# Running the seams between the dense stages of a transformer layer in two token halves, with three weight tiles taken together at the start of the next stage

## The chip, the cores and the metric

The kernel runs on one core of a Trainium2 chip. The metric is the device time of one execution in microseconds (us). TensorE (PE) multiplies, VectorE (DVE), ScalarE (ACT) and GpSimd (POOL) do the elementwise work, and SyncE (SP) issues most of the DMAs.

## The reference

One layer of a decoder for 512 prompt tokens and 8 sampled tokens, 520 in all, with a model width of 1024:

```python
hp = half_ffn(yp, *ffn1)                                    # stage a
... project(rmsnorm(hp, g_mix_pre), w_in, ...)              # 23 projection tiles
... fox_attention, nsa_attention (prompt and paged samples)
hp = hp + rmsnorm(merge_groups(o_fox, o_nsa, g_fox, g_nsa, w_out), g_mix_post)   # stage b
yp = half_ffn(hp, *ffn2)                                    # stage c

def half_ffn(x, g_pre, wg, wu, wd, g_post):
    return x + 0.5 * rmsnorm(swiglu(rmsnorm(x, g_pre), wg, wu, wd), g_post)
def swiglu(x, wg, wu, wd):
    return (silu(x @ wg) * (x @ wu)) @ wd
def rmsnorm(x, g):
    return x * rsqrt(mean(x * x) + EPS) * g
```

Everything is float32. So each dense stage ends with a norm over the whole width of its output, a sum into the residual, and a second norm ahead of the next stage's products.

## The kernel before

**Layout.** The width lies on the partitions: `H` (the residual), `Y` (a stage's output) and the operand tiles are 8 tiles (`KT`) of 128 partitions by 520 tokens (`TOK`). One matmul takes `HALF` = 260 tokens, since a PSUM bank holds 512 floats; `ps[:, 0:8]` are the eight banks, and slot n of `halves(n)` is the pair of banks 2n and 2n+1.

**Split operands.** Each float32 product is made of three: operand and weight are each split in a high and a low part (`XH`, `XL` or `UH`, `UL`; `WH`, `WL`), and `products` does, for each of the tiles `kt`, high by high, low by high and high by low, each for both halves of the tokens: 6 matmuls per `kt`, 48 for an item of eight `kt`.

**Items.** The weights come as items of 128 output columns. SP reads two items per DMA (1 MB) into `RAW`, which has two slots; ScalarE copies an item to `WH` (the high part) and VectorE subtracts to `WL` (the low part). `WH` and `WL` have two buffers each. `split(k)` is ScalarE's or VectorE's part of that for item k, and waits for semaphore `items_used` to reach k-1. SP issues a DMA when both items of the slot that it overwrites have been split by both engines. The items are counted through the program: FFN 1, the projections from `IT_PROJ` (23 items, the first of them the gates, "fg", the next four the queries, "fq"), the output projection from `IT_OUT` (8), FFN 2 from `IT_F2`.

**Order.** Each engine has its own program, written out by hand and linked by semaphores. In an FFN, gate and up items ("gu") alternate, then "down" tiles sum over the hidden units in two groups of 12 and 10; the last down tile of the second group is 2 items of 5 `kt`, 60 matmuls.

**A seam**, before the change: PE ends the last output tile (t = 7) of the stage. VectorE adds it into `Y` (in stage b three operations that scale two partial sums), ScalarE squares it (`SQ`) and scales it by the gain (`finished`), PE sums the squares of the seven earlier tiles (`ACC`) and of this one over the partitions by float32 matmuls with `ones` (`output_squares`), and ScalarE makes the token's factor of it by Ln and Exp (`rstd`, into `GT`). Then, tile by tile: VectorE `UT = Y * GT` (line 988), `H = H + UT` (line 992), ScalarE `XH` (line 668) and the square of `H` (line 670), VectorE `XL` (line 968), PE the first item's products for that `kt`, as soon as `XL` is there. The squares of `H` are summed by PE too (`first_operands`, `token_squares`), and give `token_rstd` (`R1`), by which the results of the next stage are scaled as they leave PSUM. While ScalarE and VectorE prepare, PE does 28 matmuls whose result nobody reads (`keep_warm(WARM[1])`). Behind stage c there is no next stage: `H` goes out as `y` by DMAs on ScalarE's queue.

The seams are called a (FFN 1 to projections), b (output projection to FFN 2) and c (the end).

**Start of the projections.** The gates' tile needs Sigmoid, Exp and Ln on ScalarE with a load of the function table ahead of each; ScalarE does these between the splits of items `IT_PROJ`+3 and +4, in `late_part(0)` and `softplus`.

## Time and profile before

| | |
|---|---|
| time, median of 3 runs | 1227.45 us (1222.09 to 1432.55) |
| time of the profiled execution | 1222.94 us |
| its span, first to last instruction | 1221.1 us |
| PE busy | 1171.5 us, 96% |
| DVE, ACT, POOL busy | 536.5, 419.2, 146.8 us |
| mean granted clock of TensorE | 0.978 |

The profile is of one execution. Its times are counted from the first instruction; a row of the timeline gives start, duration, engine, line, operation, what it writes and reads, and in brackets the idle time ahead of it with what ended it. `x2` joins two instructions in a row. `SPq` is SyncE's queue of DMAs. The granted clock is 1.00 at 2.4 GHz and 0.50 at 1.2 GHz.

### The profile page before, as it was taken

How to read it: one execution, taken by the hardware profiler on the slowest of the kernel's cores; microseconds unless marked ns; L12 is line 12 of the kernel's file. 1: busy time of each engine (PE TensorE's matmuls, PEld its weight loads, DVE VectorE, ACT ScalarE, POOL GpSimd, SP SyncE). 2: the span in 40 equal slices, each digit the busy share in tenths (PEclk: the TensorE clock that was granted, in tenths of full speed). 3: DMA queues.
4: the chain of work that ended last, by engine and by line, in shares of the span. 5: the costliest groups of instructions: out<-in, count | busy, mean ns of one | idle time of the engine just before them, and what ended most of it. 6: DMA issues, size and time to landing. Idle time of an engine off the chain costs nothing.

```text
span 1221.1 us, 23231 instructions
## 1 busy us (share of the span) xinstructions
PE 1171.5 (96%) x9460; PEld 1081.3 (89%) x9466; DVE 536.5 (44%) x772; ACT 419.2 (34%) x731; POOL 146.8 (12%) x150
## 2 busy tenths in 40 slices
PE   9999999999999899998979899989999999999994
PEld 6999999999999799996546556969999999999994
DVE  4433422343333644364465766574334333333334
ACT  6322322222234542234433555453223212223342
POOL 0101100001111000122212311210111000011110
PEclk9999999999999999999998898999999999999997
DMA  6322223322223133314762211222222223222221
GB/s 276 104 71 101 87 78 100 116 70 103 79 69 122 48 118 124 105 70 123 167 181 79 104 70 36 70 69 70 76 97 94 78 78 130 70 104 90 66 87 70
DMA packets 49008, 117.53 MB, mean 96 GB/s; under 512 B 8186, under 2 KB 24954, under 8 KB 43138
## 3 DMA queue, kind: packets, MB, share of 16 engines
q1 hardware_dynamic: 45746, 110.55, 27.6%
q10 hardware_dynamic: 3184, 5.88, 1.3%
q8 instruction: 56, 0.92, 0.3%
q14 instruction: 22, 0.18, 0.0%
HBM read 107.79 MB, written 7.97 MB: 95 GB/s over the span
## 4 chain that ended last, share of the span: by engine, by line
PE 91%; DVE 5%; issue 2%; ACT 2%; DMA 0%; DVEq 0%; SPq 0%; ACTq 0%
PE ps L1472 73%; PE ps L1879 4%; PE ps L1599 3%; PE ps L1632 2%; PE ps L1616 2%; PE ps L1481 2%; PE ps L1666 1%; DVE UT L988 1%; DVE H L992 1%; DVE row_max L1146 1%; PE ps L1607 1%; DVE PTS L486 1%; PE ps L1565 1%; DMA RAW<-in_w_gu 0%; ACT PRB L823 0%
## 5 line engine op out<-in xcount | busy, mean ns | idle before, releaser
L1472 PE MATMUL ps<-XH,WH 128*128 128x260 f32 x1776 | 364.2, 286 | 6.6 <-DVE XL L968 6.6
L1472 PE MATMUL ps<-XH,WL 128*128 128x260 f32 x1776 | 358.2, 283 | 0.0
L1472 PE MATMUL ps<-XL,WH 128*128 128x260 f32 x1776 | 357.7, 283 | 0.0
L417 ACT CAST WH<-RAW 128x1024 fp32r<-128x1024 f32 (+2 forms) x183 | 175.0, 956 | 519.8 <-PE ps L1472 500.5
L1472 PEld LDWEIGHTS ps<-XH,WH 128*128 128x128 f32 x1776 | 276.1, 189 | 11.1 <-DVE XL L968 8.2
L1472 PEld LDWEIGHTS ps<-XH,WL 128*128 128x128 f32 x1776 | 274.2, 189 | 0.0
L1472 PEld LDWEIGHTS ps<-XL,WH 128*128 128x128 f32 x1776 | 273.6, 189 | 0.0
L420 DVE TENSOR_TENSOR WL<-RAW,WH 128x1024 fp32r<-128x1024 f32 (+2 forms) x183 | 203.7, 1113 | 154.1 <-ACT WH L417 152.8
L1472 PE MATMUL ps<-UL,WH 128*128 128x260 f32 x704 | 141.8, 283 | 0.0
L1472 PE MATMUL ps<-UH,WL 128*128 128x260 f32 x704 | 141.5, 282 | 0.0
L1472 PE MATMUL ps<-UH,WH 128*128 128x260 f32 x704 | 141.3, 282 | 0.0
L1377 POOL TENSOR_TENSOR UL<-HT,UH 128x520 f32 (+1 forms) x44 | 57.6, 1310 | 634.2 <-ACT UH L699 634.2
L1472 PEld LDWEIGHTS ps<-UH,WL 128*128 128x128 f32 x704 | 108.5, 188 | 0.0
L1472 PEld LDWEIGHTS ps<-UH,WH 128*128 128x128 f32 x704 | 108.5, 188 | 0.0
L1472 PEld LDWEIGHTS ps<-UL,WH 128*128 128x128 f32 x704 | 108.4, 188 | 0.0
L1008 DVE TENSOR_TENSOR UT<-ps,token_rstd 128x520 f32<-128x520 f32 x44 | 30.8, 699 | 145.8 <-PE ps L1472 145.8
L1004 DVE TENSOR_TENSOR GT<-ps,token_rstd 128x520 f32<-128x520 f32 x44 | 30.8, 699 | 129.6 <-PE ps L1472 119.8
L699 ACT CAST UH<-HT 128x520 f32 (+1 forms) x44 | 27.6, 627 | 86.1 <-DVE HT L1015 86.1
L1121 DVE TENSOR_TENSOR TR<-ps,token_rstd 128x520 f32<-128x520 f32 x23 | 16.1, 700 | 68.0 <-PE ps L1472 44.6
L1146 DVE TENSOR_REDUCE row_max<-ps 128x2 f32<-128x256 f32 (+3 forms) x48 | 39.2, 817 | 11.5 <-PE ps L1607 11.4
L823 ACT ACTIVATE PRB<-ps,row_max 128x384 f32<-128x384 f32 (+1 forms) x48 | 30.0, 629 | 27.0 <-DVE row_max L1146 27.0
L486 DVE COPY PTS<-ps 128x128 f32<-128x128 f32 (+3 forms) x48 | 23.4, 488 | 31.7 <-PE ps L1616 25.9
(250 smaller groups left out, 1063.8 us busy)
## 6 DMA issues: line engine op xcount, KB each, us to landing
RAW<-in_w_gu SPq DMA_DIRECT2D x44, 1024.0 KB, 4.8
RAW<-in_w_down SPq DMA_DIRECT2D x16, 768.0 KB, 4.5
RAW<-in_w_in SPq DMA_DIRECT2D x11, 1024.0 KB, 4.8
RAW<-in_w_down SPq DMA_DIRECT2D x16, 640.0 KB, 4.3
KF<-in_fox_k SPq DMA_DIRECT2D x16, 256.0 KB, 4.2
VF<-in_fox_v SPq DMA_DIRECT2D x16, 256.0 KB, 4.0
RAW<-in_w_out SPq DMA_DIRECT2D x4, 1024.0 KB, 4.9
H<-in_x SPq DMA_DIRECT2D x4, 520.0 KB, 6.9
```

What stands on the lines that cost most here:

```text
L417: nc.scalar.copy(WH[:, par, 0:width], RAW[:, slot, j, 0:width]).then_inc(w_hi, 1)
L420: nc.vector.tensor_tensor(WL[:, par, 0:width], RAW[:, slot, j, 0:width], WH[:, par, 0:width], ALU.subtract).then_inc(w_lo, 1)
L486: copy(PTS[:, w % PT_SLOTS, 0:i + 1, :], ps[:, 4 + w % 2, 0:P * (i + 1)].rearrange("p (a n) -> p a n", n=P)).then_inc(sem(name), 1)
L699: nc.scalar.copy(row(UH, st.m), HT[:, st.par, :]).then_inc(sem("hid_hi"), 1)
L823: nc.scalar.activation(weights(v)[:, 0:W], ps[:, score_bank(v), 0:W], ACT.Exp, bias=row_max[:, v:v + 1], accum_out=row_sum[:, v:v + 1]).th ...
L1004: nc.vector.tensor_tensor(two(GT[:, st.par, :]), halves(0), two(R1[:, :]), ALU.mult).then_inc(sem("evac"), 1)
L1008: nc.vector.tensor_tensor(two(UT[:, st.par, :]), halves(1), two(R1[:, :]), ALU.mult).then_inc(sem("evac"), 1)
L1146: nc.vector.reduce_max(row_max[:, v:v + 2], ps[:, score_bank(v):score_bank(v) + 2, 0:W], AX.X, negate=True).then_inc(sem("att_max"), 1)
L1377: nc.gpsimd.tensor_tensor(row(UL, st.m), HT[:, st.par, :], row(UH, st.m), ALU.subtract).then_inc(sem("hid_lo"), 1)
L1472: q = nc.tensor.matmul(ps[:, 2 * slot + half, 0:HALF], w[:, par, cols], x[:, kt0 + kt, half * HALF:(half + 1) * HALF], start=first and kt ...
L1599: nc.tensor.matmul(ps[:, score_bank(v + j), 0:W], QX[part, h // 2, i * P:i * P + P], KX[part, k, 0:W], start=True, stop=False, skip_group_ ...
L1879: q = nc.tensor.matmul(ps[:, 2 * slot + half, 0:HALF], w[:, (IT_OUT + t) % 2, cols], x[:, kt, half * HALF:(half + 1) * HALF], start=kt % 4 ...
```

## The change

At each of the three seams the last output tile is multiplied for the first 260 tokens and then for the other 260 (before: both halves alternate). VectorE, ScalarE and PE do everything behind it for each half apart: add, square, the sum over the partitions (`half_sums`), Ln and Exp, `UT`, `H`, `XH`, square, `XL`. The next stage takes its first three items together, operand by operand: for a half h and a tile kt, nine matmuls, three for each item (`border_products`), in banks 0 to 3, 6 and 7; the items are split into three extra pairs of buffers (`EH`, `EL`), which lie where nothing lives at that time, ahead of the seam. Item +3 is split in the second half of the seam, item +4 behind it. The 28 idle matmuls at seams a and b go. `y` goes out in 16 halves on SP's queue instead of 8 tiles on ScalarE's. `OR`, `OU` and `late` move to other addresses.

```diff
+        def border(k):
+            for first in (IT_PROJ, IT_F2):
+                if isinstance(k, int) and first <= k < first + 5:
+                    return k - first
+            return None
...
             def write(k, par, slot, count, j, width):
-                if not isinstance(k, int) or k >= 2:
+                if border(k) is not None:
+                    eng.wait_ge(used, k - border(k) - (0, 0, 0, 0, 1)[border(k)] - (4 if border(k) < 3 else 0))
+                elif not isinstance(k, int) or k >= 2:
                     eng.wait_ge(used, k - 1)
...
             def behind(f, s, e):
+                if f == 1 and s.kind == "gu" and s.g == 0 and s.number == 0:
+                    return
                 if s.number is not None:
                     item(IT_F[f] + 2 * s.M + 2 + e)
+                    if f == 0 and s.M == FFN_STEPS - 1 and e == 1:
+                        item(IT_PROJ + 2)
                     return
...
@@ SyncE
-            sp.wait_ge(sem("y_stored"), 16 * KT)
+            for h in (0, 1):
+                for t in range(KT):
+                    sp.wait_ge(sem("mixed"), since("mixed", "c", h * KT + t + 1))
+                    sp.dma_start(O["y"][:, t, columns(h)], H[:, t, columns(h)]).then_inc(sem("y_stored"), 16)
...
@@ ScalarE
             def after(s, name):
-                rstd(s, "yss", 4 if s in "ac" else 1, GT[:, 0, :], "yrstd")
+                half_finished(s, 0)
+                half_rstd(s, 0, "yss", factor, GT[:, 0, :], "yrstd")
                 if name is None:
+                    half_finished(s, 1)
+                    half_rstd(s, 1, "yss", factor, GT[:, 0, :], "yrstd")
                     return
-                operands(s, name, lambda t: act.wait_ge(sem("mixed"), since("mixed", s, t + 1)))
+                for h in (0, 1):
+                    for t in range(KT):
+                        act.wait_ge(sem("mixed"), since("mixed", s, h * KT + t + 1))
+                        nc.scalar.activation(XH[:, t, columns(h)], H[:, t, columns(h)], ACT.Copy,
+                                             scale=gain(name, t)).then_inc(sem("xhi"), 1)
+                        nc.scalar.activation(Y[:, t, columns(h)], H[:, t, columns(h)], ACT.Square).then_inc(
+                            sem("hsq"), 1)
+                        if h == 0 and t == 1:
+                            half_finished(s, 1)
+                        elif h == 0 and t == 5:
+                            half_rstd(s, 1, "yss", factor, GT[:, 0, :], "yrstd")
+                        elif h == 1 and t == 3:
+                            split(first + 3)
+                        elif h == 1 and t == 5:
+                            half_rstd(s, 0, "hss", 1, R1[:, :], "rstd")
+                half_rstd(s, 1, "hss", 1, R1[:, :], "rstd")
...
             def project():
                 for j in range(NPROJ):
-                    if j + 2 < NPROJ:
+                    if 2 <= j < NPROJ - 2:
                         split(IT_PROJ + j + 2)
...
@@ VectorE
             def after(s, name):
+                last_out(s, 0)
+                for h in (0, 1):
+                    c, n = columns(h), h * KT
+                    dve.wait_ge(sem("yrstd"), since("yrstd", s, h + 1))
+                    for t in range(KT + 2):
...
+                        if h == 0 and t == 2:
+                            last_out(s, 1)
...
+                        if h == 1 and t == 7 and name:
+                            split(first + 3)
...
-            for t in range(KT):
+            for t in range(KT - 1):
                 dve.wait_ge(used, IT_OUT + t + 1)
...
                 split(IT_OUT + t + 2)
+            split(IT_F2 + 1)
+            split(IT_F2 + 2)
             after("b", "ffn2_pre")
...
@@ TensorE
+            def half_sums(s, h):
+                bank, c = ps[:, 4 + h, 0:HALF], columns(h)
+                if h == 0:
+                    pe.wait_ge(sem("acc"), since("acc", s, KT - 1))
+                pe.wait_ge(sem("ysq"), since("ysq", s, KT + h))
+                nc.tensor.matmul(bank, ones, ACC[:, c], start=True, stop=False)
+                nc.tensor.matmul(bank, ones, SQ[:, (KT - 1) % 2, c], start=False, stop=True).then_inc(sem("yss"), 1)
+            def border_products(s, first):
+                for n in range(3):
+                    ready(first + n)
+                for h in (0, 1):
+                    for kt in range(KT):
+                        pe.wait_ge(sem("xlo"), since("xlo", s, h * KT + kt + 1))
+                        for n in range(3 if h == 0 or kt < 4 else 2):
+                            q = part(n, kt, h)
+                            if h == 1 and kt == KT - 1:
+                                q.then_inc(used, 1)
+                        if kt >= KT - HSQ_PE:
+                            t = kt - (KT - HSQ_PE)
+                            nc.tensor.matmul(ps[:, 4 + h, 0:HALF], ones, Y[:, t, columns(h)], start=t == 0, stop=False)
+                        if h == 1 and kt == 2:
+                            half_token_squares(s, 0)
+                for kt in range(4, KT):
+                    q = part(2, kt, 1)
+                q.then_inc(used, 1)
+                half_token_squares(s, 1)
...
+                    if st.g == 1 and known == KT - 1:
+                        for h in (0, 1):
+                            for e in (0, 1):
...
+                                if h == 1:
+                                    q.then_inc(used, 1)
+                                    if e == 0:
+                                        half_sums(s, 0)
+                            if h == 0:
+                                q.then_inc(sem("half_done"), 1)
+                        half_sums(s, 1)
...
-            keep_warm(WARM[1])
...
             def project():
-                for j in range(NPROJ):
+                border_products("a", IT_PROJ)
+                pe.wait_ge(sem("projected"), 2)
+                turn(0)
+                for j in range(3, NPROJ):
```

What the change does to the order of the instructions, at the places where the engines wait for each other. ScalarE at seam a before; the first row is the split of the last two down items, the two `WH` rows of 1024 are `IT_PROJ` and +1, and rows 659 and 662 are Ln and Exp:

```order
L417 CAST WH<-RAW 128x640 [waits w_raw1,items_used] x2
L647 ACTIVATE SQ<-Y 128x520 [waits acc,evac]
L651 ACTIVATE Y<-Y,gains 128x520 [waits ysq]
L417 CAST WH<-RAW 128x1024 [waits w_raw0,items_used]
L647 ACTIVATE SQ<-Y 128x520 [waits acc,evac]
L651 ACTIVATE Y<-Y,gains 128x520 [waits ysq]
L417 CAST WH<-RAW 128x1024 [waits w_raw0,items_used]
L659 ACTIVATE ST<-ps,consts 128x520 [waits yss]
L662 ACTIVATE GT<-ST 128x520 [waits yss_ln]
```

ScalarE at the same place after (`EH_81`, `EH_83` and `EH_85` are the high parts of `IT_PROJ`, +1 and +2):

```order
L451 CAST WH<-RAW 128x640 [waits w_raw1,items_used] x2
L689 ACTIVATE SQ<-Y 128x520 [waits acc,evac]
L693 ACTIVATE Y<-Y,gains 128x520 [waits ysq]
L451 CAST EH_81<-RAW 128x1024 [waits w_raw0,items_used]
L451 CAST EH_83<-RAW 128x1024 [waits w_raw0,items_used]
L451 CAST EH_85<-RAW 128x1024 [waits w_raw1,items_used]
L730 ACTIVATE SQ<-Y 128x260 [waits acc,last_out]
L733 ACTIVATE Y<-Y,gains 128x260 [waits ysq]
L718 ACTIVATE ST<-ps,consts 128x260 [waits yss]
L721 ACTIVATE GT<-ST 128x260 [waits yss_ln]
```

The split of item +2 now stands ahead of the square of the last tile, and waits for another slot of `RAW` than its two neighbours. VectorE at the same place after:

```order
L454 TENSOR_TENSOR WL<-RAW,WH 128x640 [waits w_hi,items_used]
L454 TENSOR_TENSOR EL_82<-RAW,EH_81 128x1024 [waits w_hi,items_used]
L454 TENSOR_TENSOR EL_84<-RAW,EH_83 128x1024 [waits w_hi,items_used]
L454 TENSOR_TENSOR EL_86<-RAW,EH_85 128x1024 [waits w_hi,items_used]
L1072 TENSOR_TENSOR Y<-Y,ps 128x260 [waits half_done]
L1087 TENSOR_TENSOR UT<-Y,GT 128x260 [waits yg,yrstd]
L1087 TENSOR_TENSOR UT<-Y,GT 128x260 [waits yg]
L1091 TENSOR_TENSOR H<-H,UT 128x260 [waits normed]
L1087 TENSOR_TENSOR UT<-Y,GT 128x260 [waits mixed,yg]
L1091 TENSOR_TENSOR H<-H,UT 128x260 [waits normed]
L1072 TENSOR_TENSOR Y<-Y,ps 128x260 [waits items_used]
L1097 SCALAR_TENSOR_TENSOR XL<-H,gains,XH 128x260 [waits xhi]
```

The three low parts stand ahead of the sum into the last tile's first half (the first row of line 1072); the second half's is the other row of line 1072. TensorE after, at the end of the last down tile of FFN 1 and the start of the three items:

```order
L1630 MATMUL ps<-ACC,consts 128x260 [waits ysq,acc]
L1631 MATMUL ps<-SQ,consts 128x260
L1636 MATMUL ps<-UH,WH 128x260
...
L1636 MATMUL ps<-UH,WL 128x260
L1630 MATMUL ps<-ACC,consts 128x260 [waits ysq]
L1631 MATMUL ps<-SQ,consts 128x260
L1636 MATMUL ps<-XH,EH_81 128x260 [waits w_hi,w_lo,xlo]
L1636 MATMUL ps<-XL,EH_81 128x260
L1636 MATMUL ps<-XH,EL_82 128x260
L1636 MATMUL ps<-XH,EH_83 128x260
```

The sum of the first half's squares stands ahead of the last 15 of the tile's 60 matmuls, and the second half's ahead of the next stage.

## Rows read from the trace of the kernel before

**Rows 1.** The page, part 4: the chain that ended last, share by engine.

```profile
PE 91%; DVE 5%; issue 2%; ACT 2%; DMA 0%; DVEq 0%; SPq 0%; ACTq 0%
```

**Rows 2.** The chain in order of time: start, duration, what.

```profile
423.23 0.88 PE ps L1481 x4
...
428.85 51.88 PE ps L1472 x432
...
830.37 373.07 PE ps L1472 x3108
```

**Rows 3.** Timeline, seam a.

```profile
393.18 0.37 SPq L507 DMA_DIRECT2D RAW<-in_w_in  x1
...
398.21 0.40 PE L1472 MATMUL ps<-UH,WL 128*128 128x260 f32 x2
...
400.14 1.14 PE L1481 MATMUL ps<-SQ,consts 128*128 128x260 f32 x4 [0.65 <-ACT SQ L647]
...
402.41 0.64 ACT L662 ACTIVATE GT<-ST 128x520 f32<-128x520 f32 x1
403.08 1.31 DVE L988 TENSOR_TENSOR UT<-Y,GT 128x520 f32<-128x520 f32 x2
```

**Rows 4.** DMAs, KB and median us from issue to landing: 392 to 400 us, and the page.

```profile
RAW<-in_w_in SPq DMA_DIRECT2D x1, 1024.0 KB, 6.1
...
RAW<-in_w_in SPq DMA_DIRECT2D x11, 1024.0 KB, 4.8
```

**Rows 5.** Timelines of ACT and DVE, start of the projections.

```profile
429.45 0.63 ACT L730 ACTIVATE QXF<-TR 128x512 f32<-128x512 f32 x1
...
435.84 1.05 ACT L417 CAST WH<-RAW 128x1024 fp32r<-128x1024 f32 x1
...
437.00 1.23 DVE L420 TENSOR_TENSOR WL<-RAW,WH 128x1024 fp32r<-128x1024 f32 x1 [1.66 <-ACT WH L417]
```

**Rows 6.** Timelines of SP, DVE and ACT, seam b.

```profile
784.00 11.87 SPq L507 DMA_DIRECT2D RAW<-in_w_gu  x2
...
800.00 1.22 DVE L420 TENSOR_TENSOR WL<-RAW,WH 128x1024 fp32r<-128x1024 f32 x1
...
800.79 0.73 ACT L651 ACTIVATE Y<-Y,gains 128x520 f32<-128x520 f32 x1
```

**Rows 7.** Timeline, seam c.

```profile
1203.03 0.40 PE L1472 MATMUL ps<-UH,WL 128*128 128x260 f32 x2
...
1207.53 1.31 DVE L988 TENSOR_TENSOR UT<-Y,GT 128x520 f32<-128x520 f32 x2 [3.30 <-ACT GT L662]
1208.76 0.69 DVE L992 TENSOR_TENSOR H<-H,UT 128x520 f32<-128x520 f32 x1
...
1217.25 1.30 DVE L992 TENSOR_TENSOR H<-H,UT 128x520 f32<-128x520 f32 x2
```

**Rows 8.** Groups by line and form: count, busy us, mean ns, idle before.

```profile
L968 DVE SCALAR_TENSOR_TENSOR XL<-H,gains,XH 128x520 fp32r<-128x520 f32 x24 | 18.0, 757 | 2.5 <-ACT XH L668 2.3
...
L486 DVE COPY PTS<-ps 128x512 f32<-128x512 f32 x12 | 8.3, 691 | 15.4 <-PE ps L1616 15.4
...
L486 DVE COPY PTS<-ps 128x256 f32<-128x256 f32 x12 | 5.0, 417 | 1.7 <-PE ps L1616 1.7
...
L823 ACT ACTIVATE PRB<-ps,row_max 128x512 f32<-128x512 f32 x24 | 16.3, 682 | 17.1 <-DVE row_max L1146 17.1
...
L823 ACT ACTIVATE PRA<-ps,row_max 128x256 f32<-128x256 f32 x24 | 11.1, 469 | 6.1 <-DVE row_max L1146 6.0
```

**Rows 9.** Windows: length, busy PE, PEld, DVE, ACT, POOL, then PEclk, DMA share, GB/s.

```profile
412.90:416.20 3.30, 3.30 (x12) 2.91 (x13) 3.30 (x6) 2.03 (x4) 0.00 (x0) 0.50 0.00 0
...
803.80:805.90 2.10, 0.00 (x0) 0.00 (x0) 2.05 (x4) 1.06 (x2) 0.00 (x0) 1.00 0.00 0
...
1206.10:1208.20 2.10, 0.00 (x0) 0.00 (x0) 0.67 (x2) 1.33 (x2) 0.00 (x0) 1.00 0.00 0
1208.20:1221.10 12.90, 0.00 (x0) 0.00 (x0) 9.73 (x16) 0.00 (x0) 0.00 (x0) 0.50 0.43 165
```

More of the change, by code:

```diff
@@ L671, in operands, with half_rstd @@
                 rstd(s, "hss", 1, R1[:, :], "rstd")
+            def half_rstd(s, h, kind, factor, dst, done):
+                act.wait_ge(sem(kind), since(kind, s, h + 1))
+                e = 1 if factor == 4 else 0
+                nc.scalar.activation(ST[:, 0, columns(h)], ps[:, 4 + h, 0:HALF], ACT.Ln, scale=factor / D_MODEL,
+                                     bias=const("eps")[:, e:e + 1]).then_inc(sem(kind + "_ln"), 1)
+                act.wait_ge(sem(kind + "_ln"), since(kind + "_ln", s, h + 1))
+                nc.scalar.activation(dst[:, columns(h)], ST[:, 0, columns(h)], ACT.Exp, scale=-0.5).then_inc(
+                    sem(done), 1)
@@ new lines, in half_product, with part @@
+            def half_product(hi, lo, col, x, kt, bank, h, start, stop):
+                cols = slice(col * P, col * P + P)
+                for p, (w, v) in enumerate(((hi, XH if x else UH), (hi, XL if x else UL), (lo, XH if x else UH))):
+                    q = nc.tensor.matmul(ps[:, bank, 0:HALF], w[:, cols], v[:, kt, columns(h)],
+                                         start=start and p == 0, stop=stop and p == 2)
+                return q
+            def border_products(s, first):
+                tiles = [weight_tiles(first + n, None) for n in range(3)]
+                def part(n, kt, h):
+                    return half_product(*tiles[n], kt, True, kt, 2 * (0, 1, 3)[n] + h, h, kt == 0, kt == KT - 1)
+                for n in range(3):
[16 more added lines that the diff above has]
+                half_token_squares(s, 1)
@@ L1512, in ffn, with half_token_squares @@
+            def half_token_squares(s, h):
+                pe.wait_ge(sem("hacc"), since("hacc", s, h + 1))
+                nc.tensor.matmul(ps[:, 4 + h, 0:HALF], ones, Y[:, HSQ_PE, columns(h)], start=False, stop=True).then_inc(
+                    sem("hss"), 1)
             def ffn(f, before, s):
```

188 lines of the change are left out of this document (131 added, 57 removed).

## The prediction

> **What bounds the kernel now.** The chain of waits comes first: 91% of it is TensorE [rows 1], and behind each seam it runs unbroken, 432 matmuls in 51.88 us and 3108 in 373.07 us, 0.120 us each [rows 2]. So outside the seams nothing can be won, and a seam is worth what TensorE idles or does for nothing there. The reader then takes the timeline of each seam. Seam a: the last product ends at 398.6, the factor is there at 403.08, when VectorE starts on UT [rows 3], and the third item starts at 428.6, the fifth 96 matmuls later at 440.1. Seam b: TensorE stops at 803.8 [rows 9], and the 3108 matmuls hold 36 of the second item and 48 of the third, so the fourth item starts at 840.1 (the chain dates a matmul some 0.3 us behind its start). Seam c: the last product ends at 1203.4, the last H at 1218.55 [rows 7], and 2.5 us later the span ends.
>
> **Prices of half operations.** From 512 to 256 columns a VectorE copy goes from 691 to 417 ns and an ACT operation from 682 to 469 ns [rows 8]. So half of 520 columns costs 0.27 us less on VectorE and 0.22 less on ScalarE: 0.43 for UT or H (0.70 in full), 0.49 for XL. In a queue without a wait the next VectorE operation starts some 0.08 us before the last one's end, so half operations follow at 0.35 (XL 0.40). A sum over the partitions is four float32 rows in 0.88 us [rows 2], half of one is 0.44. From the end of the sums over Ln and Exp to UT it took 1207.53 - 1206.1 = 1.43 us at seam c [rows 7, 9]; with half operations 0.44 less, 1.0.
>
> **Seam a, up to the factor.** Item +2 is now split ahead of the last tile's first half, on ScalarE and on VectorE. Its DMA was issued at 393.18 [rows 3], when the last down items had been split, which the change leaves as it is; it took 6.1 us, to 399.3, where eleven of its kind have a median of 4.8 [rows 4], to 398.0. Copy 1.05 us, the low part 0.1 behind it for 1.23 [rows 5], then the half sum into Y: 402.0; the square: 402.5. The first half's 30 matmuls had ended at 395.0 and 15 more at 396.8; there TensorE stands at the sum of the squares until 402.5, with 15 matmuls queued behind. In the 12.9 us without matmuls at the end the clock was at 0.50 from 2.1 us on [rows 9], so I take it as fallen: the two half sums take 1.7 us, not 0.88. Factor at 404.2 + 1.0 = 405.2, against 403.08. The overlap that the halves would give is eaten by the split ahead of them.
>
> **Seam a, from the factor to the fifth item.** Counted from the factor: VectorE reaches the second half's sum at 1.9, ScalarE squares it behind two tiles of XH and squares at 3.15, TensorE sums until 4.1 and starts the three items. They are 144 matmuls of 0.120 (17.2), eight half sums (3.5) and two (0.9): 25.7. VectorE needs 0.35 + 0.35 + 0.40 = 1.10 us for a tile of a half where TensorE uses 1.08 to 1.5, and it starts first, so it hides behind TensorE; without that cover each 0.1 us too much costs 1.6. Then Ln and Exp (1.0) and the two full evacuations (0.62 and 0.70): 28.0. TensorE waits there for both, 2.4 us of a new wait. Then the fourth item runs, but the fifth needs ScalarE, which has the table loads of the gates' tile in front of its split: from QXF at 429.45 to the end of the low part at 438.2 it is 8.8 us [rows 5]. Before, that began early enough; now the fourth item's 5.7 and 0.5 for the turn are over at 6.2 and TensorE stands 2.7 us. The fifth item starts at 405.2 + 28.0 + 8.9 = 442.1 against 440.1: **+2.0 us**. With the landing of 4.8 and the full clock it is 2.0 - 1.3 - 0.8 = -0.1.
>
> **Seam b.** The weights for +2 were issued at 795.5 [rows 6], so the DMA is no matter. ScalarE's gain copy of tile 6 starts at 800.79 [rows 6]; behind it copies of +1 and +2, and VectorE's low parts end at 803.8 and 804.9; then three half operations to 806.15, the square to 806.6. TensorE stands at the sum from 802.3 (12 matmuls left of 48) to 806.6, and again I take the sums at the low clock, 1.7: factor at 809.3. The second half's sum is three operations, 0.45 more than at a, and nothing stands in the way of the fifth item here: the fourth starts 28.5 behind the factor, at 837.8, against 840.1: **-2.3 us**. At the full clock -3.1.
>
> **Seam c.** No weights are split. Half 0 ends at 1203.4 - 3.6 = 1199.8, its square is there before TensorE has done 15 more matmuls (1201.6); sums 1202.5, factor 1203.5, 4.0 earlier than UT at 1207.53 [rows 7]. But the tail is VectorE's: H repeats every (1217.25 - 1208.76) / 6 = 1.41 us, in halves every 1.41 - 0.54 = 0.87, and there are twice as many. 15 steps and the last H are 13.5 us: 1217.0 against 1218.55, **-1.6 us**. The DMA behind the last H is half as large and on another queue; I take its 2.5 us as they were (between -0.4 and +0.5).
>
> The Trainium skill ("VectorE: DVE Perf Modes", section "The TRN2 errata — SBUF-src ops pay a fixed extra latency per instruction") says that this latency is paid between instructions and asks for tiles of at least 512 elements, which speaks against halving. The rows show a fixed part of 0.14 us (417 ns less 256 times 1.07 [rows 8]), and the 0.87 has it in; were there none, the 16 added operations at seam c would cost 2.2 us less.
>
> **Hidden.** y on SP's queue: 16 issues of 0.37 us [rows 3] at 0.87 distance. late comes behind the second half's rstd, and is read at the eighth item only. The moved buffers cost nothing. The 28 removed matmuls lay in a wait.
>
> **The sum.** 2.0 - 2.3 - 1.6 = -1.9 us, from 1222.94 of the profiled execution: 1221.0. The clock is left: the fall at 412.9 cost 3.3 us at 0.50 [rows 9], that is 1.7 us where TensorE is the bound, and now it is from the first matmul of the three items. TensorE idles again 1.6 and 2.7 us ahead of the three items at a and b, 2.4 behind them, and 2.7 ahead of the fifth at a. Of gaps of 2.1 us one let the clock stand and one ended with it falling [rows 9]. So one such fall is as likely as none, and between 1221.0 and 1222.7 I say **1222 us**. The runs shown have 1222.09 and 1227.45 around the profiled 1222.94, so a median may lie some us above.
>
> **Rivals.**
> - *Slower: the clock.* Two to four falls instead of one, each 3.3 us at half speed on three-item products that TensorE bounds: +3.4 to +6.8 on 1221.0, 1224.4 to 1227.8. It is slower than before from the second fall on (1.9 / 1.7). For it: the keep-warm matmuls are gone and four gaps of 1.6 to 2.7 us stand in their place. Against it: the gap of 2.1 us at 803.8 left it at 1.00 [rows 9]. 0.22.
> - The Trainium skill's rule ("TensorE: Matmul & The Clock Gate", section "Why this matters for your kernels") is to leave no long idle gap between bursts of matmuls, since the array falls to half its clock; by it this rival is the likelier one.
> - *Better: early weights or full clock.* Landing as in the median and sums at 1.00: -0.1 - 3.1 - 1.6 = -4.8, 1218.1. For it: 4.8 is the median [rows 4]. Against: this very DMA took 6.1, and both gaps are over 4 us. 0.18.
> - *The halves overlap in full:* if the splits did not stand ahead, the factor would come at 398.7 at a (-4.4 for the fifth item) and 804.5 at b (-7.1), with c's -1.6: -13.1, 1210. The orders of ScalarE and VectorE speak against it. 0.04.
> - *It doesn't do what it says:* matmuls that change weights each time instead of every second one run at more than 0.120 us. 456 of them at 0.14 are +9, 1230. Against: each matmul has its own weight load already. 0.04.
>
> **How the numbers follow.** Forecast 0.50, with a range of its own of 1219 to 1225, a change of -4 to +2 us, so of either sign; 0.02 is left for what I have not thought of. 8 in 10 need the slower and the better case too: 1214 to 1229, with some us for the scatter of the runs. 2%, 24 us, is about what a measurement of this kernel can tell from no change; no case but mishaps reaches it: faster 0.02, same 0.94, slower 0.04.
>
> **What would show it.** At a: EH/EL of item +2 ends near 401.7, UT near 405, TensorE idle from 396.8 to 402.5 behind ysq, the fourth item near 433.7, the fifth at 442.1 after a wait of 2.7 us for the low part. At b: UT near 809, fourth item near 838, the granted clock at 1.00 but for the sums and one stretch at most. At c: UT at 1203.5 less what a and b gave, steps of 0.87. Wrong if XL, not TensorE, sets the pace of the three items, if item +2 lands before 396, or if the clock falls more than once.

## The result, and the profile after

The changed kernel takes 1225.49 us (median of 20 runs, 1223.04 to 1228.61) against 1223.1 us before, a ratio of 1.0025 with a 95% interval of 1.0014 to 1.0036: it is slower by 3.1 us (1.7 to 4.4), where 0.9 us faster than the profiled execution was forecast. The 1223.1 is the median of 20 runs, four of them stray ones of 1433 to 5646 us, and the ratio leaves these four out. In a second series beside other kernels the ratio was 1.0030 (1.0018 to 1.0042).

The profiled execution has a span of 1225.7 us against 1221.1, so 4.6 us are to be found in it. The chain of waits cuts the span at places that both kernels have (start, duration, what); its lines answer to those of [rows 2]:

```profile
393.24 6.41 DMA RAW<-in_w_in
...
443.69 40.60 PE ps L1590 x336
...
765.53 37.49 PE ps L2064 x312
...
846.33 356.02 PE ps L1590 x2964
```

The 336 matmuls are the fifth to the eleventh item of the projections and end at 484.29; before, the block of 432 in [rows 2] ends at 480.73 with the same item. (For the fourth item of the kernels of before I take the place 9.7 us behind the start of the 3108, where [rows 2] and 840.1 have it.) The 312 begin the output projection behind attention, the 2964 begin with the fourth item behind seam b (840.1 before). Subtracting gives four stretches, here for every profile of the study, the experiments below included; the last two columns are the time against the kernel before as measured over all runs, and its ratio with the interval. Where two kernels are compared below over all runs, it is by the difference of their ratios, and that carries both intervals: some 2.5 us either way, and 3 to 4 where one of the last two orders (six runs each) takes part.

| kernel | to item 11 (seam a) | attention | seam b | to the end (seam c) | span | all runs, us | ratio |
|---|---|---|---|---|---|---|---|
| before | 480.7 | 279.8 | 79.6 | 381.0 | 1221.1 | | |
| changed | 484.3 | 281.2 | 80.8 | 379.4 | 1225.7 | +3.1 | 1.0025 [1.0014, 1.0036] |
| changed, again | 485.6 | 281.1 | 80.8 | 379.4 | 1226.9 | +3.7 | 1.0030 [1.0018, 1.0042] |
| warm in all four waits | 483.0 | 279.3 | 77.2 | 380.7 | 1220.1 | -1.8 | 0.9985 [0.9969, 1.0001] |
| third tile split later | 479.9 | 281.2 | 78.4 | 380.9 | 1220.3 | -3.7 | 0.9970 [0.9952, 0.9988] |
| before, without warm matmuls | 481.1 | 278.2 | 78.9 | 381.0 | 1219.2 | -1.2 | 0.9990 [0.9974, 1.0005] |
| fifth item split early, first try | 484.6 | 277.7 | 79.6 | 380.7 | 1222.6 | +2.6 | 1.0021 [1.0006, 1.0035] |
| the same, second try | 482.7 | 275.8 | 79.6 | 380.9 | 1218.9 | -1.6 | 0.9987 [0.9971, 1.0003] |
| order mended | 477.2 | 279.8 | 77.1 | 379.4 | 1213.5 | -7.8 | 0.9936 [0.9912, 0.9959] |
| order mended, warm | 476.2 | 277.9 | 74.3 | 379.4 | 1207.7 | -15.4 | 0.9874 [0.9851, 0.9898] |
| seam c in full width | 483.9 | 281.3 | 80.8 | 380.9 | 1226.9 | +4.6 | 1.0038 [1.0021, 1.0054] |
| warm in b's first wait | 483.6 | 277.9 | 78.7 | 380.8 | 1221.0 | +1.1 | 1.0009 [0.9991, 1.0026] |
| warm in b's second wait | 483.9 | 277.8 | 78.1 | 379.4 | 1219.2 | +1.2 | 1.0010 [0.9996, 1.0024] |

So in the profiles seam a costs 3.6 us, seam b 1.2, seam c gives 1.6, and attention, in which the change does nothing, has 1.4 more in this execution. The predicted terms were +2.0, -2.3, -1.6, and up to 1.7 for one fall of the clock.

**Seam a.** Timelines of the changed kernel, ScalarE, VectorE and TensorE, which answer to [rows 3] (start, duration, engine, line, operation, in brackets the idle time before it and who ended it):

```profile
399.73 1.04 ACT L451 CAST EH<-RAW 128x1024 fp32r<-128x1024 f32 x1 [4.13 <-DMA RAW<-in_w_in]
402.47 0.42 ACT L730 ACTIVATE SQ<-Y 128x260 f32<-128x260 f32 x1 [1.70 <-DVE Y L1072]
...
400.87 1.23 DVE L454 TENSOR_TENSOR EL<-RAW,EH 128x1024 fp32r<-128x1024 f32 x1 [3.76 <-ACT EH L451]
402.02 0.42 DVE L1072 TENSOR_TENSOR Y<-Y,ps 128x260 f32<-128x260 f32 x1
...
403.03 1.21 PE L1630 MATMUL ps<-ACC,consts 128*128 128x260 f32 x2 [5.87 <-ACT SQ L730]
409.31 0.70 PE L1630 MATMUL ps<-ACC,consts 128*128 128x260 f32 x2 [1.13 <-ACT SQ L730]
...
406.11 0.77 DVE L1087 TENSOR_TENSOR UT<-Y,GT 128x260 f32<-128x260 f32 x2 [3.67 <-ACT GT L721]
```

Both engines stand in front of the third item's weights until 399.7. Only behind its copy and its low part comes the half sum, though the half had been multiplied at about 395; TensorE idles 5.9 us with the rest of the tile queued behind the sum. UT comes at 406.11 against 403.08 in [rows 3]. The second halves of the seam, which answer to [rows 5]:

```profile
433.12 1.43 DVE L1235 TENSOR_TENSOR TR<-ps,token_rstd 128x520 f32<-128x520 f32 x2 [4.29 <-ACT token_rstd L721]
...
442.20 1.23 DVE L454 TENSOR_TENSOR WL<-RAW,WH 128x1024 fp32r<-128x1024 f32 x1 [5.68 <-ACT WH L451]
```

VectorE waits for the factor from 428.8, evacuates, and the low part of the fifth item ends at 443.4, where the block of 336 begins.

**Seam b.** TensorE's two waits for the squares, and the granted clock in windows (length, busy PE, PEld, DVE, ACT, POOL, PEclk, DMA share, GB/s), which answer to the second window of [rows 9]:

```profile
811.66 1.20 PE L1630 MATMUL ps<-ACC,consts 128*128 128x260 f32 x2 [4.33 <-ACT SQ L730]
818.35 1.23 PE L1630 MATMUL ps<-ACC,consts 128*128 128x260 f32 x2 [2.03 <-ACT SQ L730]
```

```profile
807.30:810.80 3.50, 0.03 (x1) 0.00 (x0) 3.21 (x5) 1.10 (x2) 0.08 (x1) 0.97 0.26 35
810.80:824.20 13.40, 10.52 (x39) 9.46 (x40) 9.38 (x26) 8.84 (x22) 0.00 (x0) 0.50 0.17 70
824.20:828.00 3.80, 3.80 (x31) 3.74 (x31) 3.36 (x8) 1.46 (x5) 0.00 (x0) 0.99 0.00 0
```

This is the reading that the prediction missed. The clock falls some 1 us before the end of the first wait and stays at 0.50 for the 13.4 us of the middle window (13.6 with its edges): through the first sums and the rest of the tile, which are 4.6 us of unbroken work, the second wait, the second sums and over 4 us of the three items. It need not look like this in every execution. Both profiled ones of the changed kernel have a mean clock of 0.970, and of its 20 runs 15 have 0.973 to 0.977; another course of the clock with the same instructions is shown below, at the two waits.

**Seam c**, against [rows 7]:

```profile
1209.88 0.77 DVE L1087 TENSOR_TENSOR UT<-Y,GT 128x260 f32<-128x260 f32 x2 [3.20 <-ACT GT L721]
...
1212.12 0.42 DVE L1087 TENSOR_TENSOR UT<-Y,GT 128x260 f32<-128x260 f32 x1
...
1212.99 0.43 DVE L1087 TENSOR_TENSOR UT<-Y,GT 128x260 f32<-128x260 f32 x1
1213.33 0.42 DVE L1091 TENSOR_TENSOR H<-H,UT 128x260 f32<-128x260 f32 x1
1213.86 0.43 DVE L1087 TENSOR_TENSOR UT<-Y,GT 128x260 f32<-128x260 f32 x1
...
1222.62 0.76 DVE L1091 TENSOR_TENSOR H<-H,UT 128x260 f32<-128x260 f32 x2
```

Steps of 0.87 us (1212.12, 1212.99, 1213.86), the last H at 1223.38. Seam b's fourth item was 6.2 us later than before; 1217.0 + 6.2 = 1223.2 was forecast.

### The profile page after: what moved, and what is told of

Its sections match the earlier page's. It is cut to its first block, busy times and chain, and to the rows that moved or that the text cites. A ratio compares the mean times of both kernels' runs of the same rounds, so it can differ in the third digit from the quotient of the medians.

```text
span 1225.7 us, 23281 instructions
## 1 busy us (share of the span) xinstructions
PE 1166.3 (95%) x9410; PEld 1080.8 (88%) x9410; DVE 543.9 (44%) x845; ACT 427.3 (35%) x779; POOL 146.8 (12%) x150
## 4 chain that ended last, share of the span: by engine, by line
PE 88%; DVE 5%; ACT 2%; issue 2%; DMA 1%; DVEq 0%; SPq 0%; ACTq 0%
PE ps L1590 68%; PE ps L1636 3%; PE ps L2064 3%; PE ps L1784 2%; PE ps L1817 2%; PE ps L1801 2%; PE ps L1851 1%; DVE row_max L1262 1%; DVE UT L1087 1%; DVE PTS L524 1%; PE ps L1658 1%; PE ps L1599 1%; DVE H L1091 1%; DMA RAW<-in_w_in 1%; DVE PRB L508 1%
## 5 line engine op out<-in xcount | busy, mean ns | idle before, releaser
L1590 PE MATMUL ps<-XH,WH 128*128 128x260 f32 x1680 | 341.7, 285 | 6.0 <-DVE UT L1119 2.5
L1590 PE MATMUL ps<-XH,WL 128*128 128x260 f32 x1680 | 339.0, 283 | 0.0
L1590 PE MATMUL ps<-XL,WH 128*128 128x260 f32 x1680 | 338.6, 283 | 0.0
L1590 PEld LDWEIGHTS ps<-XH,WH 128*128 128x128 f32 x1680 | 260.3, 189 | 8.4 <-issue 5.9
L454 DVE TENSOR_TENSOR WL<-RAW,WH 128x1024 fp32r<-128x1024 f32 (+2 forms) x177 | 196.5, 1110 | 152.6 <-ACT WH L451 151.3
L1590 PEld LDWEIGHTS ps<-XH,WL 128*128 128x128 f32 x1680 | 259.6, 189 | 0.0
L1590 PEld LDWEIGHTS ps<-XL,WH 128*128 128x128 f32 x1680 | 259.0, 189 | 0.0
L1590 PE MATMUL ps<-UL,WH 128*128 128x260 f32 x664 | 133.8, 283 | 0.0
L1590 PE MATMUL ps<-UH,WL 128*128 128x260 f32 x664 | 133.4, 282 | 0.0
L1590 PE MATMUL ps<-UH,WH 128*128 128x260 f32 x664 | 133.3, 282 | 0.0
L1262 DVE TENSOR_REDUCE row_max<-ps 128x2 f32<-128x256 f32 (+3 forms) x48 | 39.1, 816 | 13.1 <-PE ps L1792 13.0
```

The lines of the kernel that those rows point to most:

```text
L454: nc.vector.tensor_tensor(lo[:, 0:width], RAW[:, slot, j, 0:width], hi[:, 0:width], ALU.subtract).then_inc(w_lo, 1)
L1262: nc.vector.reduce_max(row_max[:, v:v + 2], ps[:, score_bank(v):score_bank(v) + 2, 0:W], AX.X, negate=True).then_inc(sem("att_max"), 1)
L1590: q = nc.tensor.matmul(ps[:, 2 * slot + half, 0:HALF], w[:, par, cols], x[:, kt0 + kt, half * HALF:(half + 1) * HALF], start=first and kt ...
```

## The experiments

Theories: **L**, the clock: TensorE's work between the waits runs at half speed, and it is TensorE that sets the pace there. **S**, the split: the third weight tile stands in front of the first half's sum and eats the overlap. **W**: the wait for the fifth item behind seam a. Each experiment's edit is against the changed kernel, but for the one that starts from the kernel before. Keep-warm matmuls are products of zeros, 128x512 in bf16, into a bank that nobody reads.

### The clock: warm matmuls in all four waits

```diff
+    keep_warm(26 if f == 0 else 0)    # ahead of half_sums(s, 0)
+    keep_warm(5 if f == 0 else 0)     # ahead of half_sums(s, 1)
+    keep_warm(19)                     # ahead of half_sums("b", 0)
+    keep_warm(8, 3)                   # ahead of half_sums("b", 1)
```

> The changed kernel with keep-warm matmuls (128x512 bf16 of zeros, 0.213 us each at full clock) put into TensorE's four waits for the squares of the last tile: 26 and 5 at seam a, 19 and 8 at seam b. Theory L (the missing time is TensorE's clock, low through bursts that stand 2 to 4 us apart): granted clock 1.00 in both sets of sums and in the three items behind them, so the UT of seam a comes 0.9 us earlier and that of seam b 0.8, the second sums of seam b 0.9 earlier and the three items there end some 2 us earlier; about 5 us less than the changed kernel (1225.5), 1220 to 1221, some 2 us below the kernel before. Rival (the clock costs nothing that another wait would not take): the same as the changed kernel within 1 us.

Measured: 4.9 us less than the changed kernel (ratios 0.9985 and 1.0025, so 2.5 to 7.3), as theory L had it, and within the uncertainty of the kernel before. The chain and a window of it:

```profile
762.23 37.51 PE ps L2066 x312
...
839.39 357.36 PE ps L1590 x2964
```

```profile
804.00:820.00 16.00, 14.26 (x88) 10.38 (x87) 12.59 (x30) 10.00 (x24) 0.10 (x1) 1.00 0.20 68
```

Seam b takes 839.39 - 762.23 = 77.2 us, 3.6 less, at a clock of 1.00 throughout. Seam a gains 1.3. The block of 2964 takes 357.36 instead of 356.02: now the clock falls at the end of the wait ahead of the fourth item, in which no warm matmul stands, and 1.3 us are given back. So the seams give 4.9 us in the profile and keep 3.6 of them. Attention has 2.0 less, which need not be the warm matmuls' doing (below).

### Which of b's two waits

```diff
+    keep_warm(19)                     # one kernel: ahead of half_sums("b", 0) alone
+    keep_warm(8, 3)                   # the other: ahead of half_sums("b", 1) alone
```

> The changed kernel with keep-warm matmuls at seam b alone, 19 of them in the first wait (for the squares of the first half), none in the second. If the first gap of 4.3 us is what lets the clock fall and the short work behind it is only too little to raise it again: the granted clock is 1.00 from 804 to 820, the sums take 0.9 instead of 2.1 us and the three items run at full clock, so the fourth item comes some 3.6 us earlier than in the changed kernel, as in the run with all waits filled. If each gap counts by itself: the clock falls at the second gap of 1.5 to 2 us instead, and the gain is 1 to 2 us.

> The changed kernel with 8 keep-warm matmuls at seam b alone, in the second wait (for the squares of the second half), none in the first. If uninterrupted work raises the clock again whatever came before: it rises soon behind the second sums, and the three items gain up to 2.1 us; the first sums stay at 0.50. Rival: the low stretch lasts as long as in the changed kernel (13 us) and the gain is under 0.5 us.

The first of them, windows (columns as above):

```profile
810.00:814.40 4.40, 1.21 (x7) 0.90 (x5) 4.26 (x13) 2.98 (x7) 0.00 (x0) 0.98 0.01 2
814.40:817.70 3.30, 3.30 (x16) 3.23 (x15) 3.30 (x10) 2.53 (x8) 0.00 (x0) 0.50 0.00 0
817.70:824.00 6.30, 6.30 (x51) 6.18 (x50) 5.65 (x15) 3.88 (x12) 0.00 (x0) 1.00 0.01 4
```

and the second:

```profile
803.60:807.80 4.20, 0.00 (x0) 0.00 (x0) 3.46 (x5) 1.48 (x4) 0.01 (x1) 0.97 0.36 90
807.80:811.00 3.20, 3.12 (x10) 2.76 (x11) 0.05 (x1) 1.38 (x3) 0.00 (x0) 0.50 0.50 210
811.00:820.00 9.00, 8.08 (x57) 6.71 (x56) 8.86 (x25) 6.60 (x17) 0.00 (x0) 1.00 0.01 2
```

With the first wait filled the clock stands there. It falls just behind the second wait, which had grown to 3.2 us since the rest of the tile now ran at full speed; the low window is 3.3 us. Seam b gains 2.1 us, but the clock falls once more at the fourth item (the block of 2964 takes 357.50), which gives 1.4 back. With the second wait filled the low window is 3.2 us, b gains 2.7, and nothing is given back.

This looks as if the second gap had held the clock down in the changed kernel. The rows do not bear that out. The first of the eight warm matmuls starts behind the rise of the clock at 811.0 (TensorE's timeline):

```profile
811.75 1.90 PE L1606 MATMUL ps<-cumb 128*128 128x512 bf16 x8
```

Up to there the instructions are those of the changed kernel, whose clock stayed down through the same burst. And the two kernels with the fifth item split early (below) have the changed kernel's instructions at seam b, without any warm matmul, and almost its waits. Windows of the first of them:

```profile
808.10:811.30 3.20, 2.89 (x9) 2.54 (x10) 0.00 (x0) 1.43 (x4) 0.00 (x0) 0.50 0.55 233
811.50:814.70 3.20, 0.91 (x8) 0.70 (x6) 3.06 (x9) 1.71 (x5) 0.00 (x0) 1.00 0.01 3
815.00:818.20 3.20, 3.10 (x10) 2.71 (x11) 3.20 (x10) 2.54 (x7) 0.00 (x0) 0.50 0.00 0
```

The clock rises in the first burst, falls again at the end of the second wait, and a third time at the fourth item (357.52 for the 2964). So the same order has had one low stretch of 13.6 us, in three profiles (the changed kernel twice and the one with seam c in full width, 80.8 us at b each), and three short ones, in two profiles (79.6 each). From the start of the 312 to the last instruction both come to the same: 460.2 us for both profiles of the changed kernel, 460.3 and 460.5 for the other two. What decides between them is open. What the filled waits show is their price: over the same stretch 457.9 us with both filled, 459.5 with the first alone, 457.4 with the second alone. Over all runs the two kernels are 2.0 and 1.8 us below the changed kernel, or 2.6 and 2.4 below its repetition beside them. Their ratios do not tell them apart.

### The split in front of the first half

```diff
 def behind(f, s, e):
-    if f == 0 and s.M == FFN_STEPS - 1 and e == 1:
-        item(IT_PROJ + 2)
 # ScalarE, after(), behind half_rstd(s, 0, "yss", ...)
+    split(first + 2)
 # VectorE, after(), behind last_out(s, 1)
+    if name:
+        split(first + 2)
 # both engines, ahead of after("b", ...)
-    split(IT_F2 + 2)
```

> The changed kernel with the third weight tile of each border split behind the first half instead of ahead of it: on ScalarE right behind the Exp of the first half, on VectorE behind the second half sum. Theory S (the split ahead of the first half ate the overlap): UT of seam a at 399.8 to 400.5 instead of 406.1, of seam b some 4.9 us earlier; the fifth item of seam a 5 to 6 us earlier; together 8 to 11 us less than the changed kernel, 1214 to 1217. Rival (the three items only start when the third tile is there and VectorE is late with its low halves, since 2.3 us of split stand among them): less than 4 us of gain, with TensorE idle behind the third tile or behind XL.

VectorE's and TensorE's timelines at seam a:

```profile
400.12 0.77 DVE L1085 TENSOR_TENSOR UT<-Y,GT 128x260 f32<-128x260 f32 x2 [2.71 <-ACT GT L719]
...
398.00 0.68 PE L1629 MATMUL ps<-ACC,consts 128*128 128x260 f32 x2 [0.92 <-ACT SQ L728]
403.32 1.13 PE L1629 MATMUL ps<-ACC,consts 128*128 128x260 f32 x2 [2.41 <-ACT SQ L728]
```

At seam a UT comes at 400.12, 6.0 us earlier: theory S holds. Of these 6.0, 4.4 are left at the eleventh item, 2.4 us come at seam b, and 1.5 are lost at the fourth item behind it, where the clock falls once more; over all runs it is 6.7 us less than the changed kernel, short of the 8 to 11. At b my 4.9 was wrong: VectorE's low part of the second item still waited for ScalarE's copy in front of the half sum, and UT came only 1.3 us earlier, counted from the 312. The missing 1.6 us at a are the clock again. The changed kernel spends its low stretch on the last 15 matmuls of the tile, in front of a wait; here it falls just behind the wait of 2.41 us and lies on the second sums (1.13 for two that take 0.70) and the first of the three items, where TensorE is the bound.

### The warm matmuls that the change removed

```diff
     ffn(0, "0", "a")
-    keep_warm(WARM[1])
...
-    keep_warm(WARM[1])
     ffn(1, "b", "c")
```

> The kernel before without its two sets of 28 keep-warm matmuls behind the sums. Theory L (their absence lets the clock fall): the first items behind the seams run at 0.50 for a stretch of at least 3 us, +1.5 to +4 us on the kernel before. Rival (they lay in a wait and cost nothing to remove): within 1 us of it.

Measured 0.9990, 1.2 us less than the kernel before with an interval from -3.2 to +0.6: their removal has no cost that shows. Yet the clock falls, and for long (a window, columns as above, and rows of TensorE's timeline in it):

```profile
403.80:416.60 12.80, 8.72 (x31) 7.47 (x32) 12.70 (x22) 8.19 (x14) 0.00 (x0) 0.50 0.24 82
```

```profile
409.07 0.80 PE L1472 MATMUL ps<-XH,WH 128*128 128x260 f32 x2 [0.16 <-DVE XL L968]
410.96 0.80 PE L1472 MATMUL ps<-XH,WH 128*128 128x260 f32 x2 [0.22 <-DVE XL L968]
412.85 0.80 PE L1472 MATMUL ps<-XH,WH 128*128 128x260 f32 x2 [0.22 <-DVE XL L968]
```

Here VectorE is busy for 12.70 of the 12.80 us, TensorE for 8.72: it takes a tile of operands when VectorE brings one, every 1.89 us, and has time left even at 0.50. The third item starts at 429.24 against 428.85 in [rows 2]. In the changed kernel a low stretch on the three items does cost, since TensorE has three items for each operand there and is busy without a pause: the change took away the slack in which a slow clock had been free.

### The wait for the fifth item

```diff
 # ScalarE, project(): ahead of the wait for the first evacuation
-    if 2 <= j < NPROJ - 2:
+    if j == 0:
+        split(IT_PROJ + 4)
+    elif 3 <= j < NPROJ - 2:
         split(IT_PROJ + j + 2)
 # VectorE, project(): ahead of the first evacuation, instead of behind the third
+    split(IT_PROJ + 4)
```

> The changed kernel with the fifth projection item split ahead of the gates' tile: on ScalarE before it waits for the first evacuation, on VectorE before it makes it. Theory W (the fourth item is followed by a wait of about 2.7 us for the fifth item's low part, behind the table loads of the gates' tile): that wait goes and the fifth item starts 2 to 2.7 us earlier; 2 to 3 us less than the changed kernel, 1222.5 to 1223.5. Rival (ScalarE's later work, the evacuation of the gates' tile or the sixth item, becomes late instead): within 1 us of the changed kernel.

No gain (1.0021). On ScalarE the copy stood behind the last Exp, VectorE's low part behind the copy, and the first evacuation behind that:

```profile
433.91 1.22 DVE L454 TENSOR_TENSOR WL<-RAW,WH 128x1024 fp32r<-128x1024 f32 x1 [5.17 <-ACT WH L451]
435.05 1.43 DVE L1238 TENSOR_TENSOR TR<-ps,token_rstd 128x520 f32<-128x520 f32 x2
```

It came 1.9 us later than at 433.12, so the wait went from the fifth to the fourth item. The second try puts it into the idle time in front of the Ln:

```diff
 # ScalarE, after(): ahead of the last half_rstd(s, 1, "hss", ...)
+    if s == "a":
+        split(first + 4)
 # VectorE, after(): ahead of the wait for its result
+    if s == "a":
+        split(first + 4)
```

> As the experiment on the fifth item, but with its split in the stretch where both engines idle behind the three items: on ScalarE ahead of the last Ln and Exp of the token sums (it idles some 4.6 us there), on VectorE ahead of the wait for that factor. Theory W: the first evacuation stays where it is in the changed kernel, the fourth item too, and the wait of 2.7 us for the fifth goes: 2 to 2.7 us less than the changed kernel. Rival (ScalarE's table loads hold up the evacuation of the gates' tile or the sixth item instead, or the slower clock behind the gap bounds the fourth and fifth items): less than 1 us.

Its chain, and a window behind the gap:

```profile
435.01 47.64 PE ps L1592 x384
```

```profile
435.80:438.80 3.00, 3.00 (x16) 3.00 (x16) 0.47 (x1) 2.94 (x6) 0.00 (x0) 0.50 0.94 385
```

The evacuation is in its place (432.87) and the fourth and fifth item stand in one block of 384, so the wait is gone. But 384 matmuls at 0.120 us are 46.1 and this took 47.64: for over 3 us of the fourth item the clock was at 0.50, in the changed kernel too (435.1 to 438.6), where the wait for the fifth hid it. The eleventh item ends 1.6 us earlier, not 2.7. Over all runs the kernel is 4.6 us below the changed one, more than seam a shows; the rest I can only place in attention (275.8 in this profile), and whether it would stay there is open.

### Seam c in full width

The last output tile of the second FFN, its sums, UT, H and the storing of y are again as before, on SP's queue in 8 pieces:

```diff
-    if st.g == 1 and known == KT - 1:
+    if st.g == 1 and known == KT - 1 and f == 0:
...
-    for h in (0, 1):
-        for t in range(KT):
-            sp.wait_ge(sem("mixed"), since("mixed", "c", h * KT + t + 1))
-            sp.dma_start(O["y"][:, t, columns(h)], H[:, t, columns(h)]).then_inc(sem("y_stored"), 16)
+    for t in range(KT):
+        sp.wait_ge(sem("mixed"), since("mixed", "c", t + 1))
+        sp.dma_start(O["y"][:, t, :], H[:, t, :]).then_inc(sem("y_stored"), 16)
```

> The changed kernel with seam c as it was before: the last output tile and the tail behind it in full width, y stored in 8 pieces from SP's queue. If term c (-1.6 by the prediction, -1.4 as I read it in the profile) is right: 1.4 to 1.6 us more than the changed kernel, the last H some 1.5 us later. Rival (the half tail's doubled operations eat what the earlier factor gives): no difference.

The last stretch takes 380.9 us instead of 379.4: in the profiles term c holds. Over all runs it is 1.6 us more (1.0038 against 1.0025), which agrees but is not clear of the noise.

### All of it together, the clock cold and warm

In the first of the two VectorE has no late weight tile in front of a half sum any more: the third tile at a as above, at b VectorE's second and third behind the first half sum, and the fifth item of the projections as in the second try. ScalarE's copies at b stay in front of the square.

```diff
 # VectorE, after(), behind last_out(s, 0)
+    if s == "b":
+        split(first + 1)
+        split(first + 2)
 # VectorE, ahead of after("b", ...)
-    split(IT_F2 + 1)
-    split(IT_F2 + 2)
```

> The changed kernel with no split of weights in front of a half sum: at seam a the third item is split behind the first half, at seam b VectorE takes the second and third item behind the first half sum, and the fifth projection item is split behind the three items. Theory S with W: seam a as in the run with the third tile split later (the fifth item 4.4 us earlier), 2 to 2.7 us for the fifth item, and some 1.2 us at seam b on top: 9 to 11 us less than the changed kernel, about 1215. Rival (the wait only moves, to the low clock behind each gap): 6.7 us less at most, as that run alone.

The second adds keep-warm matmuls to it, 4 and 10, 8 and 10 ahead of the half sums, and behind the three items:

```diff
     border_products("a", IT_PROJ)
+    pe.wait_ge(sem("hss_ln"), since("hss_ln", "a", 1))
+    keep_warm(10, 4)
...
     border_products(before, k)
+    pe.wait_ge(sem("hss_ln"), since("hss_ln", before, 1))
+    keep_warm(8, 4)
```

> The last one with keep-warm matmuls in TensorE's waits: 4 and 10 ahead of the two half sums at seam a, 8 and 10 at seam b, and 10 and 8 between the three items and the fourth. Theory L: the granted clock stays at 1.00 through both seams, and the sums and the three items gain another 2 to 4 us at seam b and 1 to 2 at seam a: 3 to 5 us less than the run without them, about 1211. Rival (with the order mended VectorE and not TensorE sets the pace of the three items, so the clock is worth little): within 1 us of it.

The first is 10.9 us below the changed kernel, as expected, and UT of seam b comes 3.7 us earlier, counted from the 312; with the warm matmuls it is 18.5 us below it, and at 0.9874 (0.9851 to 0.9898) 15.4 us faster than the kernel before. Chain and windows of the second:

```profile
430.05 46.10 PE ps L1595 x384
...
754.00 37.48 PE ps L2075 x312
...
828.33 356.02 PE ps L1595 x2964
```

```profile
396.00:444.00 48.00, 47.30 (x346) 42.31 (x345) 34.54 (x70) 31.15 (x65) 0.00 (x0) 1.00 0.27 94
796.00:845.00 49.00, 47.28 (x349) 42.89 (x346) 33.12 (x69) 26.87 (x55) 2.66 (x2) 1.00 0.19 66
```

The granted clock is 1.00 through both seams. From the one to the other the profile gains 1.1 us at a, where the clock had stood at 1.00 until the fourth item anyway, and 2.8 at b: 3.9 of the expected 3 to 5. All runs show 7.6, with six runs of each kernel and an uncertainty of about 4; the rest is not seen at the seams (attention has 1.9 less in this pair of profiles).

### The changed kernel again

> The changed kernel unchanged, beside the others and for a second profile. If the stretch between the seams (attention, whose code and data are the same in all) differs by chance of the clock: another value between 276 and 281.5 us for it, seam a as before (the fifth item about 3.5 us later than in the kernel before), and a ratio of 1.002 to 1.004.

The chain:

```profile
443.73 41.88 PE ps L1590 x336
...
766.72 37.49 PE ps L2064 x312
```

Seam a repeats to 0.1 us at the fifth item, and so does b (80.8). The expectation spoke of the fifth item alone; behind it the 336 matmuls took 1.3 us more here, so at the eleventh item seam a costs 4.9 us in this profile. For attention there are now five profiles of kernels that are the same, instruction by instruction, up to seam b: 281.2, 281.1, 281.3, 277.9 and 277.8 us, mean 279.9 against 279.8 before. So the 1.4 us of the profile need be no effect of the change: the stretch takes one of several times. The two profiled executions also took longer than most runs of the kernel (1227.5 and 1228.7 us against medians of 1225.5 and 1225.6). By this the profile has 4.6 us where all runs have 3.1, and the three terms alone, 3.6 + 1.2 - 1.6 = 3.2, fit the runs; that is argued from these few profiles, not shown.

## Why the prediction was wrong

**Right.** Where the kernel is bound and that the overlap is eaten by the splits ahead of the halves: the factor was forecast at 405.2 and 809.3 (with the 5.0 us by which b came later, 814.3) and came at 406.1 and 814.7; with the split moved it came at 400.1. That half-order matmuls stay at 0.120 us: 336 in 40.60 is 0.121. That TensorE and not XL sets the pace of the three items. The wait for the fifth item: 1.1 us of it are idle time, and 1.5 went into the fourth item's matmuls at half speed, together the 2.7 that were forecast, but not as they were forecast. Term c, -1.6, in the profile and, within its noise, by its own experiment. That the removed 28 matmuls lay in a wait: without them the kernel before is not slower.

**Slightly off.** Term a was +2.0 and measured +3.6 at the eleventh item, +3.3 at the fifth. UT was 0.9 late: 0.35 from the DMA, which took 6.4 us (6.1 forecast), and the rest from the way over the half sum, the sums and the factor. From UT to the second evacuation it took 28.4 instead of 28.0. With term b's first part, 0.4, these are 1.7 us.

**Wrong.** The step that failed is the paragraph on the clock under the sum: "one such fall is as likely as none", with 3.3 us at 0.50 for each, and, in term b, the low clock taken for the first sums only. I had read the length of a low stretch from a place where TensorE then worked without a pause [rows 9], and carried it to places where the work is in bursts. At b the clock fell in the gap of 4.3 us, and a burst of 4.6 us, a gap of 2.0 and 6 us of the next burst went by before it rose: 13.6 us at 0.50, of which the second sums (0.9) and over 4 us of the three items (2.1) were on the path. Term b was -2.3 and is +1.2, 3.5 us off; with the warm matmuls in the two waits it is -2.4, where the prediction's own price at full clock was -3.1. In other executions of the same order the clock fell three times for a short stretch instead, with the same time to the end, so that the course of the clock varies and its cost hardly does; in no profile of this order did it come down to one short stretch beside the first sums, and "if the clock falls more than once" was the prediction's own sign of being wrong. The rival "slower: the clock" described this, and its 1224.4 to 1227.8 holds the result. The rival of the full overlap, 1210, was not in this change, but with the order mended (and the fifth item's split moved with it) 7.8 of its 13.1 us are there, and the rest only with the clock up. The chance of 0.22 for the clock was too small, because I weighed against it one gap of 2.1 us that had left the clock alone, although both first waits are over 4 us long, the condition under which I had myself taken the clock as fallen.

The rule of the Trainium skill that stood beside this rival ("TensorE: Matmul & The Clock Gate", section "Why this matters for your kernels"), not to leave long idle gaps between bursts of matmuls, is borne out by the kernels with filled waits (-4.9 us, and in the last -7.6). The kernel before without its warm matmuls shows where it is worth nothing: a low clock for 12.8 us and no cost that shows, where VectorE is the bound.

**Open.** Attention takes between 275.8 and 281.3 us with the same instructions in it. Whether seam b has one long low stretch or three short ones is not settled either. Two kernels, the second try on the fifth item and the last one, gain 3 us more over all runs than their seams show, which is about the uncertainty of the comparison; I cannot say whether it is noise, this scatter or an effect of the seams on the stretch behind them.

## What to carry to other kernels

Before a chain is cut into halves so that one half hides behind the other, look at what else stands in the queues in front of the first half's small operations: a weight split of 2.3 us there, with the wait for its DMA, held the factor up by 6.0 us, and with it moved behind them the kernel was 3.7 us faster than before instead of 3.1 slower. A change that removes the slack of TensorE makes the clock count: price the low clock over the whole run of bursts and waits, up to the next uninterrupted stretch, and not by the length of one low stretch read elsewhere. And before a low stretch is put down to a wait, look for a second execution of the same order: here two of them had the clock fall at other places. And when a wait is taken away, ask whether it had been hiding a slow stretch: here 1.5 of 2.7 us came back as matmuls at half speed.

## What the runs showed of the hardware

- With the same instructions and waits of 4.3 and 2.0 to 2.7 us at seam b the granted clock has stayed at 0.50 for 13.6 us, with TensorE busy for 10.6 of them and once for 4.6 us without a pause, and has fallen for three short stretches (windows of 3.2, 3.2 and 3.0 us are wholly at 0.50). The time from the start of the output projection to the end was 460.2 to 460.5 us in both cases.
- Equal waits need not have equal ends. The kernel with the third tile split later and the one with the order mended have the same instructions up to there and the same waits of 0.92 and 2.40 us at seam a: in the first the clock fell just behind the second wait, in the other, in this window, it stood at 1.00 until the fourth item:

```profile
396.00:430.00 34.00, 28.08 (x205) 26.10 (x204) 27.50 (x62) 21.57 (x50) 0.00 (x0) 1.00 0.18 59
```

- The DMA of the third and fourth projection weights took 6.41, 6.24, 6.08, 6.08, 6.07, 5.97 and 5.74 us to land in seven profiles of kernels in which the third item's split waits for it, where the median of the eleven of its kind is 4.8 to 5.1: the 6.1 of the kernel before was no accident of one profile. Why this place is slower is open.
